# One product per token tile for the meta keys of all heads in the attention of a two-layer decoder trunk

## The reference

```python
def causal_block_attention(q, k, v):        # T = 272, 8 heads, 96 wide q and k, 64 wide v
    bounds = [0, 16, 144, 272]
    for s, e in zip(bounds[:-1], bounds[1:]):
        sc = einsum('bqhd,bkhd->bhqk', q[:, s:e], k[:, :e]) * scale
        mask = arange(e)[None, :] <= arange(s, e)[:, None]
        p = softmax(where(mask, sc, -1e30), axis=-1)
        outs.append(einsum('bhqk,bkhd->bqhd', p, v[:, :e]))
```

## Time and profile before

| what | value |
|---|---|
| time, median of 3 runs | 1084.81 us (1083.55 to 1088.18) |
| the profiled execution, its own time | 1082.41 us |
| its span in the trace | 1080.6 us |
| granted TensorE clock, mean | 0.921 of full speed |
| busy PE / PEld / DVE / ACT / POOL | 1002.3 / 880.7 / 732.2 / 575.5 / 29.5 us |
| attention of layer 0, from the first score to the output projection | 131.7 to 206.7 us of the span |
| attention of layer 1, the same | about 544.5 to 609 us |

### The profile page before, as it was taken

How to read it: one execution, slowest core, us unless ns; L and a number is a source line. 1 busy time by engine, 2 the same in 40 slices (tenths; PEclk the granted TensorE clock), 3 DMA queues, 4 the chain that set the end, 5 groups by cost and what they waited for, 6 DMA issues and landing times.

```text
span 1080.6 us, 15923 instructions
## 1 busy us (share of the span) xinstructions
PE 1002.3 (93%) x5963; PEld 880.7 (82%) x5963; DVE 732.2 (68%) x982; ACT 575.5 (53%) x789; POOL 29.5 (3%) x58
## 2 busy tenths in 40 slices
PE   5988977999999999997977999999999999999995
PEld 3963755899999999873565889999989898989894
DVE  5645564366666565554564456998989798979994
ACT  4473152254545343444162236777777877787762
POOL 4130000000000000000000000000000000000000
PEclk9998865799999999998875769999999999999998
DMA  8411201055557763401311133998999899989981
GB/s 257 155 39 61 58 23 56 3 183 166 181 168 201 197 191 108 153 9 40 117 52 66 53 114 108 357 347 305 356 343 347 299 358 361 328 318 357 348 316 41
DMA packets 120019, 203.76 MB, mean 189 GB/s; under 512 B 5874, under 2 KB 73740, under 8 KB 119964
## 3 DMA queue, kind: packets, MB, share of 16 engines
q1 hardware_dynamic: 119504, 202.80, 55.0%
q10 hardware_dynamic: 460, 0.23, 0.1%
HBM read 201.97 MB, written 1.05 MB: 188 GB/s over the span
## 4 chain that ended last, share of the span: by engine, by line
PE 83%; DVE 10%; ACT 3%; issue 2%; DMA 0%; ACTq 0%; DVEq 0%
PE ps L2105 20%; PE ps L564 11%; PE ps L566 10%; PE ps L565 10%; PE ps L2130 10%; PE ps L1900 4%; PE ps L1716 3%; DVE wlo L1174 3%; PE ps L1791 2%; PE ps L2063 2%; PE ps L1822 1%; PE ps L1891 1%; PE ps L1836 1%; PE ps L1721 1%; ACT whi L806 1%
## 5 line engine op out<-in xcount | busy, mean ns | idle before, releaser
L1174 DVE TENSOR_TENSOR wlo<-raw,whi 128x1536 fp32r<-128x1536 f32 (+4 forms) x296 | 437.3, 1506 | 94.1 <-ACT whi L806 91.6
L806 ACT ACTIVATE whi<-raw 128x1536 fp32r<-128x1536 f32 (+4 forms) x296 | 376.0, 1284 | 164.2 <-PE ps L566 86.5
L564 PE MATMUL ps<-uhi,whi 128*128 128x272 f32 (+1 forms) x576 | 171.1, 297 | 2.9 <-DVE ulo L1192 2.9
L566 PE MATMUL ps<-uhi,wlo 128*128 128x272 f32 (+1 forms) x576 | 168.9, 293 | 0.0
L565 PE MATMUL ps<-ulo,whi 128*128 128x272 f32 (+1 forms) x576 | 168.6, 293 | 0.0
L2105 PE MATMUL ps<-whi,xeh 128*128 128x320 f32 (+1 forms) x512 | 124.5, 324 | 0.0
L2105 PE MATMUL ps<-wlo,xeh 128*128 128x320 f32 (+1 forms) x512 | 123.4, 322 | 0.0
L2105 PE MATMUL ps<-whi,xel 128*128 128x320 f32 (+1 forms) x512 | 123.3, 322 | 0.0
L564 PEld LDWEIGHTS ps<-uhi,whi 128*128 128x128 f32 (+1 forms) x576 | 110.7, 192 | 9.3 <-issue 8.8
L565 PEld LDWEIGHTS ps<-ulo,whi 128*128 128x128 f32 (+1 forms) x576 | 110.8, 192 | 0.0
L566 PEld LDWEIGHTS ps<-uhi,wlo 128*128 128x128 f32 (+1 forms) x576 | 110.5, 192 | 0.0
(11 more groups left out here) (279 smaller groups left out, 1411.0 us busy)
## 6 DMA issues: line engine op xcount, KB each, us to landing
raw<-in_moe_w_down_dram SPq DMA_DIRECT2D x24, 1536.0 KB, 7.9
raw<-in_moe_w_gate_dram SPq DMA_DIRECT2D x16, 1536.0 KB, 7.8
raw<-in_moe_w_up_dram SPq DMA_DIRECT2D x16, 1536.0 KB, 8.3
raw<-in_moe_w_gate_dram SPq DMA_DIRECT2D x16, 1280.0 KB, 7.6
raw<-in_moe_w_up_dram SPq DMA_DIRECT2D x16, 1280.0 KB, 6.8
raw<-in_ffn_w_gate_dram SPq DMA_DIRECT2D x11, 1024.0 KB, 5.3
raw<-in_ffn_w_up_dram SPq DMA_DIRECT2D x11, 1024.0 KB, 5.3
raw<-in_ffn_w_down_dram SPq DMA_DIRECT2D x8, 1408.0 KB, 7.2
```

The source lines that it names most:

```text
L564: pe.matmul(dst, wh, xh, start=start, stop=False, skip_group_check=True)
L566: return pe.matmul(dst, wl, xh, start=False, stop=stop, skip_group_check=True)
L806: act.activation(placed(whi, s, src), src, ACT.Copy).then_inc(hi_done, 1)
L1174: dve.tensor_tensor(placed(wlo, s, src), src, placed(whi, s, src).bitcast(F32), ALU.subtract).then_inc(lo_done, 1)
```

## The change

The 16 meta keys of all 8 heads, 8 x 16 = 128 columns of weights, are gathered side by side and turned by one transpose; one product of 128 rows and 512 columns adds their part for all heads. For it `vt[:, 0, :]` holds, on partition 16h + n, the values of meta key n in the 64 columns of head h, and zeros elsewhere.

- POOL copies the latent columns of the meta tokens 8 times side by side (`ckvm`), so that the values' matmul of tile 0 gives the meta values on all 128 partitions; ACT copies 128 partitions; POOL multiplies them by a constant mask (`C_OWN`) into the block-diagonal form.
- POOL copies the meta weights of all heads of a tile together into `pm`, after the tile's last exponential.
- `values(t)` makes for each head only the transposes and products of key tiles 1 and 2, all into bank 5 with one start, and then a ninth item, `META`: one transpose, one DVE copy, one product of 512 columns. For tile 0 it makes only this item.
- Per head one copy is left of two. DVE's order in layer 0 becomes `turned(0, META)`, `averages(0)`, `gelu_times`, `maxima(2)`.

```diff
@@ -264,6 +267,19 @@
 TURN_A, TURN_B = ((1, 4, 3), (0, 2, 4)), ((1, 4, 4), (0, 1, 5))
 
 
+META = NH
+
+
+def items(t):
+
+    return (META,) if t == 0 else tuple(range(NH + 1))
+
+
+SUMS0, _k = {}, 0
+for _l in range(DEPTH):
+    for _t in tiles(_l):
+        SUMS0[_l, _t] = _k
+        _k += len(items(_t)) - 1
 POWERS, _k = {}, 0
 for _l in range(DEPTH):
     for _name in [("att", _t) for _t in tiles(_l)] + ["n2"] * _l:
@@ -346,6 +362,8 @@
 
         pT = sb("pT", [P, 2, 3 * P], to=mixer)
         osb = sb("osb", [P, 2, DH2], to=mixer)
+        pm = kr[:, :, :].rearrange("p a t -> p (a t)")[:, DH2:DH2 + 2 * P].rearrange("p (a n) -> p a n", a=2)
+        ckvm = osb[:, 1, P:P + KVC * P].rearrange("p (k n) -> p k n", k=KVC)
         mixer.close()
 
         other = ExitStack()
@@ -754,8 +775,24 @@
             pool.wait_ge(vec_done, 2)
 
             for l in range(DEPTH):
+                pool.wait_ge(lat_done, 5 * l + 5)
+                many = ckv[:, :, 0:NMETA].rearrange("p k (o n) -> p k o n", o=1).to_broadcast([P, KVC, NH, NMETA])
+                pool.tensor_copy(ckvm.rearrange("p k (h n) -> p k h n", h=NH), many).then_inc(spread_done, 1)
+                pool.wait_ge(spread_done, l + 1)
+                b = B[l, "v", 0]
+                pool.wait_ge(emptied[b.bank], b.before + 1)
+                own = con[:, C_OWN:C_OWN + NH].rearrange("p (h o) -> p h o", o=1).to_broadcast([P, NH, VH])
+                v0 = vt[:, 0, :].rearrange("p (h d) -> p h d", h=NH)
+                pool.tensor_tensor(v0, v0, own, ALU.mult).then_inc(v0_done, 1)
+                pool.wait_ge(v0_done, l + 1)
                 for t in tiles(l):
-                    power(rv[0:TILES[t][1], t:t + 1])
+                    m = TILES[t][1]
+                    turn = len(tiles(0)) * l + tiles(l).index(t)
+                    pool.wait_ge(exp_done, NH * (turn + 1))
+                    pool.tensor_copy(pm[0:m, t % 2, :].rearrange("p (h n) -> p h n", h=NH), scores[t][0:m, :, 0:NMETA])\
+                        .then_inc(pm_done, 1)
+                    pool.wait_ge(pm_done, turn + 1)
+                    power(rv[0:m, t:t + 1])
                 if l:
                     power(rv[:, 3:5])
 
@@ -936,8 +973,7 @@
                     act.activation(ksq[r, h, :], bank(b, r), ACT.Square).then_inc(emptied[b.bank], 1)
                 mark().then_inc(ksq_done, 1)
                 for t in range(3):
-                    n = TILES[t][1]
-                    take(B[l, "v", t], vt[0:n, t, :], rows=slice(0, n), cols=slice(0, DH2))
+                    take(B[l, "v", t], vt[:, t, :], cols=slice(0, DH2))
 
                 act.wait_ge(s_done, l + 1)
                 act.activation(ta[:, :, :], ta[:, :, :], ACT.Sqrt, scale=0.25).then_inc(root_done, 1)
@@ -964,17 +1000,12 @@
 
                 def turned(t, h):
 
-                    n = TILES[t][1]
-                    k0 = tiles(l).index(t)
                     b = B[l, "p", t, h]
                     act.wait_ge(filled, b.ready())
 
                     if h >= 2:
-                        act.wait_ge(pv_done, (NH - 1) * (len(tiles(0)) * l + k0) + h - 1)
-                    q = act.activation(pT[0:NMETA, 1, 0:n], ps[0:NMETA, b.bank, 0:n], ACT.Copy)
-                    if t:
-                        q = act.activation(pT[:, 1, P:(t + 1) * P], ps[:, b.bank, P:(t + 1) * P], ACT.Copy)
-                    q.then_inc(emptied[b.bank], 1)
+                        act.wait_ge(pv_done, SUMS0[l, t] + h - 1)
+                    act.activation(pT[:, 1, 0:t * P], ps[:, b.bank, 0:t * P], ACT.Copy).then_inc(emptied[b.bank], 1)
 
                 def out_high(t):
                     lead, n = TILES[t]
@@ -995,7 +1026,8 @@
                     for h in range(NH):
                         exponential(t, h)
                         if k0 and h % 2:
-                            turned(tl[k0 - 1], h)
+                            if tl[k0 - 1]:
+                                turned(tl[k0 - 1], h)
                             if t == 2:
                                 mix(l, N_IN + h // 2)
                     if k0 == 0:
@@ -1328,16 +1360,13 @@
 
                 def turned(t, h):
 
-                    n = TILES[t][1]
                     b = B[l, "p", t, h]
+                    cols = t * P if h < META else TILES[t][1]
                     dve.wait_ge(filled, b.ready())
 
-                    if h >= 2:
-                        dve.wait_ge(pv_done, (NH - 1) * (len(tiles(0)) * l + tiles(l).index(t)) + h - 1)
-                    q = dve.tensor_copy(pT[0:NMETA, 0, 0:n], ps[0:NMETA, b.bank, 0:n])
-                    if t:
-                        q = dve.tensor_copy(pT[:, 0, P:(t + 1) * P], ps[:, b.bank, P:(t + 1) * P])
-                    q.then_inc(emptied[b.bank], 1)
+                    if t and h >= 2:
+                        dve.wait_ge(pv_done, SUMS0[l, t] + h - 1)
+                    dve.tensor_copy(pT[:, 0, 0:cols], ps[:, b.bank, 0:cols]).then_inc(emptied[b.bank], 1)
 
                 def averages(t):
 
@@ -1410,11 +1439,9 @@
                 maxima(tl[1])
                 gelu_inner()
                 if l == 0:
-                    for h in range(0, NH, 2):
-                        turned(0, h)
-                        if h == 2:
-                            gelu_times()
+                    turned(0, META)
                     averages(0)
+                    gelu_times()
                     maxima(2)
                     normed(0)
                 for h in range(0, NH, 2):
@@ -1422,6 +1449,7 @@
                     if l and h == 2:
                         gelu_times()
                     mix(l, N_IN + h // 2)
+                turned(1, META)
                 if l == 0:
                     out_low(0)
                 averages(1)
@@ -1436,6 +1464,7 @@
                         dve.engine_nop().then_inc(emptied[B[l, "rnbc"].bank], 1)
                     if h == 4:
                         rn_low()
+                turned(2, META)
                 averages(2)
                 normed(2)
                 out_low(2)
@@ -1831,9 +1860,12 @@
                 for t, (lead, m) in enumerate(TILES):
                     b = B[l, "v", t]
                     fill(pe, b)
+                    if t == 0:
+                        pe.wait_ge(spread_done, l + 1)
                     for k in range(KVC):
                         wv = wkv[:, k, :].rearrange("p (h d) -> p h d", h=NH)[:, :, NOPE:]
-                        q = pe.matmul(ps[0:m, b.bank, :].rearrange("p (h d) -> p h d", h=NH), ckv[:, k, lead:lead + m], wv,
+                        at = ckv[:, k, lead:lead + m] if t else ckvm[:, k, :]
+                        q = pe.matmul(ps[:, b.bank, :].rearrange("p (h d) -> p h d", h=NH), at, wv,
                                       start=(k == 0), stop=(k == KVC - 1))
                     q.then_inc(filled, 1)
 
@@ -1880,26 +1912,38 @@
                 def values(t):
                     lead, n = TILES[t]
                     turn = len(tiles(0)) * l + tiles(l).index(t)
+                    o = B[l, "o", t].bank
+                    its = items(t)
                     fill(pe, B[l, "o", t])
-                    for h in range(NH + 1):
-                        if h < NH:
+                    for i in range(len(its) + 1):
+                        if i < len(its):
+                            h = its[i]
                             b = B[l, "p", t, h]
                             fill(pe, b)
-                            pe.wait_ge(exp_done, NH * turn + h + 1)
-                            for j in range(t + 1):
-                                kl, kn = TILES[j]
-                                q = pe.transpose(ps[0:kn, b.bank, j * P:j * P + n], scores[t][0:n, h, kl:kl + kn], ident[0:n, 0:n])
+                            if h == META:
+                                pe.wait_ge(pm_done, turn + 1)
+                                q = pe.transpose(ps[:, b.bank, 0:n], pm[0:n, t % 2, :], ident[0:n, 0:n])
+                            else:
+                                pe.wait_ge(exp_done, NH * turn + h + 1)
+                                for j in range(t):
+                                    kl = NMETA + j * P
+                                    q = pe.transpose(ps[:, b.bank, j * P:(j + 1) * P], scores[t][0:n, h, kl:kl + P], ident)
                             q.then_inc(filled, 1)
-                        if h:
-                            g = h - 1
+                        if i:
+                            g = its[i - 1]
                             b = B[l, "p", t, g]
 
                             pe.wait_ge(emptied[b.bank], b.before + 1)
-                            for j in range(t + 1):
-                                kn = TILES[j][1]
-                                q = pe.matmul(ps[0:n, B[l, "o", t].bank, g * VH:(g + 1) * VH], pT[0:kn, g % 2, j * P:j * P + n],
-                                              vt[0:kn, j, g * VH:(g + 1) * VH], start=(j == 0), stop=(j == t))
```

(21 more changed lines are left out.)

## The result

The changed kernel takes 1068.14 us (median of 4 runs, 1067.43 to 1068.87) against 1086.29 for the kernel before (4 runs, 1083.55 to 1088.18): ratio 0.9829, 95% interval 0.9810 to 0.9848.

The account below looks back on a forecast made before the run. PE was taken as the bound for 83% of the span. Layer 0 saves 1.6 + 2.5 + 3.0 = 7.1, layer 1 0.1 + 3.0 = 3.1, together 10.2 us: median 1074.6 us, range 1069.5 to 1080.

Parts of the forecast that it names:

- Values 2, both layers: Second values stage, PE-bound: three fewer records a head, less the new transpose and product, save 3.0 us a layer.
- Values 1, layer 0: First values stage: ACT becomes the bound, the new item's copy queues behind DVE's fourth split; 2.5 us saved.
- Values 1, layer 1: Same stage and queue, with gelu_times in it: 0.1 us saved, bounds -0.3 and +0.9.
- Tile 0, layer 0: Eight transposes, products and copies become one each; scores 2 end 1.6 us earlier, bounds 0 and 2.4.
- The long product: New item's product of 512 columns: two records of 0.86 us, 1.72 at the lower clock level.
- (d): Tile 0: POOL's gather can't run beside gelu_inner's multiply; term 1.2 instead of 1.6, time up to 1075.4; chance 0.24.
- (b): Output projection and long products: the clock rises sooner, up to 5 us more saved, 1069.6; chance 0.13.
- (a): Only values 2 pays; values 1 of layer 0 and tile 0 give nothing: 6.0 us or less, 1078.8; chance 0.19.
- (c): Thinner PE work keeps the clock at 0.50 longer into the output projection: slower, 1086.2; chance 0.04.
- Costed at nothing: POOL's spread and masking, tile 0's wider values' matmul, ACT's 128-partition copies, later gathers, later recurrence result: 0 us.

Follow-up runs that it names:

- e1: Kernel before, with the meta keys' products of tiles 1 and 2 over 128 rows instead of 16, zero rows added: 1073.75 us, ratio 0.9898.
- e5: Kernel before, with the meta keys' products of tiles 1 and 2 over 64 rows instead of 16: 1086.54 us (one run).
- e6: Kernel before, with each 16-row product of tiles 1 and 2 issued twice in a row: 1092.5 us (one run).
- e9: Changed kernel, with DVE's copy of the new item moved ahead of the last split of values 1: 1066.51 us, ratio 0.9815 to the kernel before.
- e10: Changed kernel, with gelu_times put back ahead of averages(0) in layer 0: 1065.18 us, ratio 0.9798 to the kernel before.
- e8: Changed kernel, with the new 512-column product issued as eight of 64 columns: 1079.35 us, ratio 0.9927 to the kernel before.
- e7: Changed kernel, with gelu_inner's multiply of layer 0 held until POOL's gather is done: 1067.12 us (one run).

## Why the prediction was wrong

**Values 2, both layers** is the step that failed: "a record costs 0.22 us and each head 0.33 more", and with it "A 16-row record of the meta keys thus costs as much as a 128-row one." Both came from comparing heads that all had 16-row products in them. The 0.33 went with the change of rows (e1, e5, e6), so without 16-row products a head costs 6 x 0.195 = 1.17 us, not 1.66. The term was 3.0 us a layer and measured 6.7, to the end of the long product (7.3 by the first load of the output projection). Of the 3.7 missed, the heads make 3.6 (eight times 0.49, less the 0.3 for which the first head still waits for its copy); the new transpose without its 0.33 gives 0.3, and the long product takes 0.2 back (1.91 against 1.72). The idle mark stood on the 16-row load itself in the earlier trace rows ("16*128 ... [0.33 <-DVE pT]"), and was read as a wait for the copy. In values 2 before, the same mark names no copy from the second head on:

```profile
181.09 1.54 PEld L1900 LDWEIGHTS ps<-vt,pT 16*128 16x128 f32 x6 [0.33 <-issue]
```

**Values 1, layer 0** was right: 2.5 forecast, 2.3 measured. The copy is late behind the fourth split, as said; e9 shows the price of that queue, 1.3 us in this layer.

**Values 1, layer 1** was right: 0.1 and 0.1. The same queue hides the shorter work of PE; e9 gains 1.6 there.

**Tile 0, layer 0**: the steps were right in their order, but 0.2 came of 1.6 in the pair, 0.5 on average over the profiles named under the table. The working did not give 1.6 either: ends at 148.2 to 149.4 save 1.2 to 2.4, and less the 0.8 for the gather that is 0.4 to 1.6. The 1.6 is the end for the upper level and not for a mixed clock, and the scores ran at 0.50. Against the forecast's own steps, counted from the first score, the product starts at 7.6 us (forecast 7.1 without the gather's delay), averages start at 9.6 (8.9), gelu_times ends at 13.6 (13.0), and the last maximum's end is at 18.8 (17.4): half a microsecond from the late transpose, 0.2 from the product, and most of the rest from maxima that wait for PE at the lower level ("[0.40 <-PE ps L1909]"). The order written out by hand makes it a term at all: gelu_times behind the averages cost 2.3 us (e10).

**The long product**: 1.72 forecast for two records; 1.9 at tile 0, 2.0 in values 1 and 1.9 in values 2. That is a little more than two records of the values' matmul, which the prediction had named as a sign against it; it costs 0.2 to 0.3 us an item. e8 shows that the one long product is cheaper than eight short ones.

**Rivals.** (d), the port, was right as a fact: the gather and the multiply don't run side by side at full speed, 1.26 us against 0.28, and POOL's power takes 1.50 beside gelu_times. This is what the Trainium skill, "SBUF — State Buffer", section "SBUF: two separate sides", has as an exclusive lock; the trace agrees: the gather ends at 141.87, 0.15 us behind the multiply. Its price was near the 0.4 that (d) gave: DVE's copy waits 0.58 us for the late transpose, and the product starts 0.5 us later than with DVE as the bound. No run takes this price away by itself, since e7 holds the multiply instead. (b), the clock, came in part: behind the long product the output projection has none of the lower level in layer 0 and 1.4 us in layer 1, where it had 3.8 and 4.1, and the two blocks gain 1.6 and 1.2; but the long products stayed at 0.50. What decides when the level rises stays open: e1 and e8 have neither stops nor long products in values 2, and their output projections run low for 2.3 and 2.0 us (e1) and for 5.0 and 5.2 (e8). Of (a) the part on tile 0 came, where the gather and the late gelu_times took most of the gain; values 1 of layer 0 paid, so its price did not. (c) did not come.

**Costed at nothing** held for POOL's spread, the masking and the copies. What was not seen is the layout: the eight columns of constants cost 2.6 us in a stage that the prediction called untouched. The sum of the named terms was 10.2; they measured 16.0 in the pair (0.2 + 2.3 + 6.7 + 0.1 + 6.7). The clock's share (1.6 and 1.2 in the output projections, up to 2.0 ahead of the experts) comes on top, and the layout's 2.6 and the 1.0 ahead of layer 1 go off it.

## What to carry to other kernels

Before costing a small matmul, look whether it stands between others of another row count: here a 16-row product among 128-row ones cost half a microsecond a head at the lower level, and filling it up with zero rows alone gained 1%. An idle mark on a record is to be tried against both readings (what it waits for, and what shape it is) before it becomes a fixed price of the loop. A change that widens a tensor allocated early moves all that follow: compare PE's busy time in an untouched stage, for the same number of records.

## What the runs showed of the hardware

- Switching between products over 16 or 64 rows and over 128 cost PE 0.49 us for each switch and back at clock 0.50 (2.30 against 1.81 a head), of which 0.33 shows as an idle mark; a further 16-row record cost 0.21. Whether it costs as much at the upper level was not measured.
- Moving the tensors by 32 bytes made the same 2277 PE records busy 3.4 us longer (397.24 to 400.66), and a record of 512 columns 398 ns instead of 393. A shift by 64 bytes cost 1.5 us more in that stage (410.4 against 408.9). Which tensor's place does it was not tried.
- Eight products of 64 columns in place of one of 512 cost 1.7 us in values 2 (13.64 against 11.93), and the output projection behind them stayed at 0.50 for 5.0 and 5.2 us.
- A GpSimd copy of 16x128 took 0.28 us alone and 1.26 beside a VectorE multiply of two SBUF operands; a 16x1 power 0.57 with VectorE on scores out of PSUM and 1.50 beside gelu_times.
